# Modulation sums of two transformer layers moved from VectorE to GpSimd, gate columns made stationary, and up-projections of 512 columns

## The reference

```python
c_act = jax.nn.silu(c)
for l in range(DEPTH):                                   # 2
    mod = c_act @ w_mod[l] + b_mod[l]                    # [1024] @ [1024, 6144]
    shift1, scale1, gate1, shift2, scale2, gate2 = split(mod, 6)
    h = rms_norm(x, norm1) * (1.0 + scale1) + shift1
    proj = h @ w_in                                      # pooling, queries, keys, values, 24 gate columns
    mix = concat([pool_mixer(u), nsa_mixer(q, k, v, gates)]) @ w_out
    x = x + gate1 * mix
    h2 = rms_norm(x, norm2) * (1.0 + scale2) + shift2
    x = x + gate2 * (square(relu(h2 @ w_ff1)) @ w_ff2)   # 1024 -> 4096 -> 1024
```

## Time and profile before

| what | value |
|---|---|
| median of 3 runs (lowest, highest) | 1443.71 us (1436.76, 1446.1) |
| profiled execution | 1444.85 us, span 1443.2 us |
| mean granted clock of PE | 0.917 |
| heads of layer 0, and its feed-forward loop | about 125 to 197 us, 260 to 420 us |
| the same of layer 1 | about 520 to 586 us, 650 to 815 us |
| second block | from about 822 us |

### The profile page before, as it was taken

The page is one execution under the profiler, slowest core; times in us unless marked ns, Lnnn a source line. Parts: engine busy times, 40 slices in busy tenths (PEclk is TensorE's granted clock), DMA queues, the critical chain, the costliest instruction groups (busy, mean ns, idle before and its releaser), DMA issues.

```text
span 1443.2 us, 23428 instructions
## 1 busy us (share of the span) xinstructions
PE 1336.0 (93%) x9578; PEld 1228.0 (85%) x9578; DVE 920.0 (64%) x1435; ACT 629.1 (44%) x935; POOL 36.5 (3%) x39
## 2 busy tenths in 40 slices
PE   6798889999999987899999999898879999799997
PEld 6785468999998854789999998788759998799996
DVE  5747854677766579556544747987784753645553
ACT  3433213444435333144444444458876632644442
POOL 1012000000000120000000000000000000000000
PEclk8788659999999887799999999899979999899999
DMA  9451522676743515245555563336654361455540
GB/s 383 138 198 59 204 88 88 233 296 231 296 167 134 200 60 211 80 184 207 174 178 190 217 213 128 99 138 218 219 175 174 119 221 42 169 188 193 179 145 30
DMA packets 43626, 247.75 MB, mean 172 GB/s; under 512 B 4160, under 2 KB 12368, under 8 KB 15520
## 3 DMA queue, kind: packets, MB, share of 16 engines
q1 hardware_dynamic: 43104, 244.57, 47.4%
q0 software_dynamic: 448, 2.14, 0.4%
HBM read 245.58 MB, written 1.11 MB: 171 GB/s over the span
## 4 chain that ended last, share of the span: by engine, by line
PE 67%; DVE 14%; issue 12%; DMA 3%; ACT 3%; POOL 1%; SPq 0%; POOLq 0%; DVEq 0%; ACTq 0%
PE bank L331 20%; PE bank L332 19%; PE bank L333 19%; DVE arena L823 3%; DVE w_lo L326 2%; PE bank L407 2%; DVE arena L1662 1%; DVE arena L950 1%; DMA arena<-dscr 1%; DMA arena<-in_modw 1%; POOL arena L341 1%; ACT w_hi L321 1%; PE bank L1273 1%; PE bank L1316 1%; DMA cst<-in_cst 1%
## 5 line engine op out<-in xcount | busy, mean ns | idle before, releaser
L326 DVE TENSOR_TENSOR w_lo<-raw,w_hi 128x2048 fp32r<-128x2048 f32 x170 | 389.7, 2295 | 240.3 <-ACT w_hi L321 240.2
L331 PE MATMUL bank<-act_hi,w_hi 128*128 128x256 f32 x1568 | 467.2, 298 | 19.6 <-DVE act_lo L844 12.6
L332 PE MATMUL bank<-act_lo,w_hi 128*128 128x256 f32 x1568 | 455.4, 290 | 0.0
L333 PE MATMUL bank<-act_hi,w_lo 128*128 128x256 f32 x1568 | 454.8, 290 | 0.0
L321 ACT ACTIVATE w_hi<-raw 128x2048 fp32r<-128x2048 f32 x170 | 324.3, 1910 | 217.0 <-PE bank L333 117.4
L331 PEld LDWEIGHTS bank<-act_hi,w_hi 128*128 128x128 f32 x1568 | 312.7, 199 | 33.6 <-issue 28.5
L332 PEld LDWEIGHTS bank<-act_lo,w_hi 128*128 128x128 f32 x1568 | 313.9, 200 | 1.1 <-issue 1.0
L333 PEld LDWEIGHTS bank<-act_hi,w_lo 128*128 128x128 f32 x1568 | 313.0, 200 | 0.0
L331 PE MATMUL bank<-ff_hi,w_hi 128*128 128x256 f32 (+1 forms) x816 | 232.2, 285 | 2.9 <-DVE ff_lo L1046 1.9
L333 PE MATMUL bank<-ff_hi,w_lo 128*128 128x256 f32 (+1 forms) x816 | 231.4, 284 | 0.0
L332 PE MATMUL bank<-ff_lo,w_hi 128*128 128x256 f32 (+1 forms) x816 | 231.3, 283 | 0.0
(11 more groups left out here) (281 smaller groups left out, 1581.2 us busy)
## 6 DMA issues: line engine op xcount, KB each, us to landing
raw<-in_panels SPq DMA_DIRECT2D x170, 1024.0 KB, 4.9
arena<-in_modw SPq DMA_DIRECT2D x48, 1024.0 KB, 6.7
mixf<-dscr SPq DMA_DIRECT2D x8, 512.0 KB, 5.7
arena<-dscr SPq DMA_DIRECT2D x8, 512.0 KB, 4.6
mixf<-dscr SPq DMA_DIRECT2D x8, 256.0 KB, 6.1
...
arena<-in_x SPq DMA_DIRECT2D x1, 1024.0 KB, 5.2
```

What stands on the lines that cost most here:

```text
L326: nc.vector.tensor_tensor(w_lo[slot(k)][:, :], raw[:, k % RAW, :], w_hi[slot(k)][:, :].bitcast(F32), ALU.subtract).then_inc(lo_done, 1)
L331: nc.tensor.matmul(o, wh, xh, start=start, stop=False, skip_group_check=skip)
L332: nc.tensor.matmul(o, wh, xl, start=False, stop=False, skip_group_check=skip)
L333: return nc.tensor.matmul(o, wl, xh, start=False, stop=stop, skip_group_check=skip)
```

## The change

Three edits. The modulation sums of both layers (not the three pairs ahead of layer 0) go to POOL: four products of 512 columns in place in the unit, one add of 1024 columns, one of 512, and for a second half one more of 512. POOL's loop over layers is written out, and the sums stand behind `pool_window` in its program. The gate columns become the stationary operand, are copied to SBUF, and turned back by two transposes. Up-projections keep `act_hi` and `act_lo` side by side (`act2`), so that `w_hi` meets both in one matmul of 512 columns, and half `c` now has a bank of its own; ACT copies the cross part, DVE adds it to the other part, and takes ReLU and square in one instruction.

```diff
@@ -105,7 +105,8 @@
         w_hi = [sb(f"w_hi{i}", [P, PANEL], F32R) for i in range(SPLIT)]
         w_lo = [sb(f"w_lo{i}", [P, PANEL], F32R) for i in range(SPLIT)]
         x = sb("x", [P, KC, T])
-        act_hi, act_lo = sb("act_hi", [P, KC, T], F32R), sb("act_lo", [P, KC, T], F32R)
+        act2 = sb("act2", [P, KC, 2, T], F32R)
+        act_hi, act_lo = act2[:, :, 0, :], act2[:, :, 1, :]
 
         with nc.sbuf_tensor("mixf", [P, 2 * KC * T], F32) as mixf:
             pass
...
         ff_full = sem("ff_full")
-        ff_relu = sem("ff_relu")
+        ff_cross = sem("ff_cross")
+        ff_sum = sem("ff_sum")
         ff_sq = sem("ff_sq")
         ff_his = sem("ff_his")
         ff_ready = sem("ff_ready")
...
 
+        def pool_mods(pool, l, link):
+
+            for n in range(6):
+                for half in range(2):
+                    pool_mod(pool, 12 * l + 4 + n, mod_sums[:, 2 * n:2 * n + 2, :], half, link)
+
+            for pair in range(12 * l + 10, 12 * l + 16 if l + 1 < layers else 12 * l + 12):
+                pool.wait_ge(macc_free, 2 * pair + 2)
+                for half in range(2):
+                    pool_mod(pool, pair, macc[:, :, :], half, link)
+
+        def pool_mod(pool, pair, o, half, link):
+
+            pool.wait_ge(modraw[half], 16 * pair)
+            unit = modw[:, half, :].rearrange("p (b k n) -> p b k n", b=2, k=4)
+            for k in range(4):
+                kc = 4 * half + k
+                ins = nc.gpsimd.tensor_scalar(unit[:, :, k, :], unit[:, :, k, :], cact[:, kc:kc + 1], None, ALU.mult)
+            link(ins)
+            link(nc.gpsimd.tensor_tensor(unit[:, :, 0:2, :], unit[:, :, 0:2, :], unit[:, :, 2:4, :], ALU.add))
+            if half == 0:
+                nc.gpsimd.tensor_tensor(o, unit[:, :, 0, :], unit[:, :, 1, :], ALU.add).then_inc(mod_used, 1)
+            else:
+                link(nc.gpsimd.tensor_tensor(unit[:, :, 0, :], unit[:, :, 0, :], unit[:, :, 1, :], ALU.add))
+                pool.wait_ge(mod_used, 2 + 2 * pair + 1)
+                nc.gpsimd.tensor_tensor(o, o, unit[:, :, 0, :], ALU.add).then_inc(mod_used, 1)
+
         def pe_gfree(pe, l, g):
...
             pe.wait_ge(gw_lo, l + 1)
-            for tt in range(TT):
-                for kc in range(KC):
-                    ts = slice(tt * P, (tt + 1) * P)
-                    last = mm3(G(3)[:, tt * 24:(tt + 1) * 24], act_hi[:, kc, ts], act_lo[:, kc, ts], gwh[:, kc, :], gwl[:, kc, :],
-                               kc == 0, kc == KC - 1)
+            for kc in range(KC):
+                last = mm3(G(3)[0:24, 0:T], gwh[:, kc, :], gwl[:, kc, :], act_hi[:, kc, :], act_lo[:, kc, :], kc == 0, kc == KC - 1)
             last.then_inc(gfull, 1)
             pe_gfree(pe, l, 4)
             pe_used(pe, pe_panel(pe, m, L_Q0, G(4), act_hi, act_lo))
+            pe.wait_ge(gfree[1], 7 * l + 3)
+            for tt in range(TT):
+                last = nc.tensor.transpose(bank[3][:, 24 * tt:24 + 24 * tt], gf[0:24, tt * P:(tt + 1) * P], ident[0:24, 0:24])
+            last.then_inc(g_turned, 1)
             turn(0)
 
             pe.wait_ge(tb_lo, l + 1)
...
 
-                pe.wait_ge(ff_relu, jn + 1)
-                last = pe_panel(pe, mm, k, bank[4 + par], act_hi, act_lo, arr)
+                pe.wait_ge(lo_done, 4 * mm + k + 1)
+                wh, wl = w_hi[slot(k)], w_lo[slot(k)]
+                for c in range(2):
+                    pe.wait_ge(ff_sum, 2 * jn + c + 1)
+                    for kc in range(KC):
+                        if c == 0 and arr:
+                            arr(kc)
+                        s = kc * 256 + c * P
+                        nc.tensor.matmul(bank[4 + c][:, :], wh[:, s:s + P], act2[:, kc, :, :], start=kc == 0, stop=False)
+                        last = nc.tensor.matmul(bank[4 + c][:, 0:T], wl[:, s:s + P], act_hi[:, kc, :], start=False, stop=kc == KC - 1)
+                    if c == 0:
+                        last.then_inc(ff_full, 1)
                 pe_used(pe, last)
 
             def down(mm, k, jn, par, first, final):
...
             act.wait_ge(gfull, 3 * l + 1)
-            nc.scalar.activation(gts[:, :, :], G(3)[:, 0:48].rearrange("p (t n) -> p t n", t=TT), ACT.Exp, scale=-1.0).then_inc(gfree[1], 1)
+            nc.scalar.activation(gf[0:24, :], G(3)[0:24, 0:T], ACT.Copy).then_inc(gfree[1], 1)
             used(L_Q0)
             nc.scalar.activation(tbuf[:, 2:4, :], G(4)[:, :].rearrange("p (b t) -> p b t", b=2), ACT.Square).then_inc(nr_sq, 1)
+            act.wait_ge(g_turned, l + 1)
+            nc.scalar.activation(gts[:, :, :], bank[3][:, 0:48].rearrange("p (t n) -> p t n", t=TT), ACT.Exp, scale=-1.0).then_inc(gate_e, 1)
             split_hi(act, m, 7)
 
             def roots(*js):
...
             def step(mm, jn, kf, par, kd, s, at):
-
-                act.wait_ge(split_free, SPLIT + 4 * mm + kf + 1)
-
                 act.wait_ge(ff_ready, jn + 1)
-                nc.scalar.activation(fr[par], bank[4 + par][:, :], ACT.Relu).then_inc(ff_relu, 1)
+                for c in range(2):
+                    if c == 0:
+                        act.wait_ge(ff_full, jn + 1)
+                    else:
+                        act.wait_ge(split_free, SPLIT + 4 * mm + kf + 1)
+                    nc.scalar.activation(fr[par][:, c * T:(c + 1) * T], bank[4 + c][:, T:2 * T], ACT.Copy).then_inc(ff_cross, 1)
                 if s[0] is not None:
                     split_hi(act, mm, s[0])
                 act.wait_ge(ff_sq, jn + 1)
...
 
-            dve.wait_ge(gfree[1], 7 * l + 3)
+            dve.wait_ge(gate_e, l + 1)
             link(nc.vector.tensor_scalar(gts[:, :, :], gts[:, :, :], 1.0, None, ALU.add))
             link(nc.vector.reciprocal(gts[:, :, :], gts[:, :, :]))
             link(nc.vector.tensor_scalar(gts[:, 0, 0:24:3], gts[:, 0, 0:24:3], cst[:, C_VALID:C_VALID + 1], None, ALU.mult))
...
 
-            def mod(half, steps=(0, 8)):
-
-                pair = half // 2
-                dve_mod(dve, 12 * l + 4 + pair, mod_sums[:, 2 * pair:2 * pair + 2, :], half % 2, steps=steps)
-
             maxima(0)
             maxima(1)
             weigh(0)
@@ -980,8 +1023,6 @@
                     split_lo(dve, m, 11)
                 if i + 2 < 8:
                     maxima(i + 2)
-                for half in ((0,), (1, 2), (3,), (4, 5), (6,), (7, 8), (9,), (10, 11))[i]:
-                    mod(half)
                 if i >= 2 and i % 2 == 0:
                     mixed((i - 2) // 2)
             mixed(3)
@@ -1004,7 +1045,7 @@
                     nc.vector.scalar_tensor_tensor(x[:, kc, :], bank[4 + i % 2][:, c * T:(c + 1) * T], modc[:, 16 + kc:17 + kc], x[:, kc, :],
                                                    ALU.mult, ALU.add).then_inc(x_ready, 1)
             dve_norm(dve, 2 * l + 1, KC, 24)
-            dve_ff(dve, m, L_FF, 16 * l, l=l, mods="ahead" if ahead else "tail")
+            dve_ff(dve, m, L_FF, 16 * l)
 
             if ahead:
                 dve.wait_ge(macc_free, 2 + 24 * l + 32)
...
-                dve_mod(dve, pair, macc, half)
+        def dve_ff(dve, m, k0, j0, final=False):
 
             def step(mm, jn, kf, par, kd, s, at):
-                dve.wait_ge(ff_relu, 2 + jn + 1)
-                nc.vector.tensor_tensor(fr[par], fr[par], fr[par], ALU.mult).then_inc(ff_sq, 1)
+                for c in range(2):
+                    dve.wait_ge(ff_cross, 2 * jn + c + 1)
+                    nc.vector.tensor_tensor(fr[par][:, c * T:(c + 1) * T], bank[4 + c][:, 0:T], fr[par][:, c * T:(c + 1) * T], ALU.add).then_inc(ff_sum, 1)
+                dve.wait_ge(ff_sum, 2 * jn + 4)
+                nc.vector.scalar_tensor_tensor(fr[par], fr[par], 0.0, fr[par], ALU.max, ALU.mult).then_inc(ff_sq, 1)
                 if s[0] is not None:
                     split_lo(dve, mm, s[0])
                 dve.wait_ge(ff_his, jn + 1)
                 nc.vector.tensor_tensor(ff_lo[:, par, :], fr[par], ff_hi[:, par, :].bitcast(F32), ALU.subtract).then_inc(ff_ready, 1)
-                mod(at, par)
                 if s[1] is not None:
                     split_lo(dve, mm, s[1])
 
...
         @block.gpsimd
         def _(pool):
-            link = Chain(pool, pool_links, 7)
+            link = Chain(pool, pool_links, 0)
 
             pool.dma_start(ccol[:, :], a["ccol"]).then_inc(c_loaded, 16)
             nc.gpsimd.memset(ub, 0.0)
             nc.gpsimd.memset(wb[0], 0.0)
             link(nc.gpsimd.memset(wb[1], 0.0))
-            link.first = link.n
-            with pool.Fori(0, layers) as l:
-                link.layer(l)
-
+            for l in range(layers):
                 pool.wait_ge(x_ready, 16 * l + 8)
                 pool.dma_start(lc[:, :], a["lcs"][l]).then_inc(lc_ready, 16)
                 pool_rope(pool, l)
                 pool_window(pool, l, link)
-                link.end()
+                pool_mods(pool, l, link)
             pool_second(pool)
 
         @block.tensor
```

17 lines of the change are left out of this document (5 added, 12 removed).

## The result

The changed kernel takes **1626.39 us** (median of four runs, 1619.79 to 1628.28) against 1444.9 us (1436.76 to 1448.04): the ratio is 1.1258, with a 95% interval of 1.12 to 1.1315. I had forecast 1475 us, range 1440 to 1540. The sign was right; the size was six times mine, 183 us of span (1443.2 to 1626.5) against 30.

What follows compares the result with a forecast made beforehand. PE was taken to bound the feed-forward, and the last modulation sum to decide when the heads' output projection starts. From 1444.85 us, 47 + 8 - 18 + 1 - 8 = +30 gave 1475 us, range 1440 to 1540.

Steps and rivals of the forecast that it cites:

- The price of the product: POOL's one-input product of 512 columns in the modulation sums: 0.78 us, between the memset's 0.48 and the in-place add's 1.27.
- A: Rival: POOL products at the memset's rate, loads setting 12 us a pair, kernel not slower, 1439 us; chance 0.20.
- The attention term: Heads of both layers: PE waits for POOL's last modulation sum, +19.6 us in layer 0 and +27.4 in layer 1, together +47.
- What I added for contention: Heads: DVE's instructions hold up POOL's sums, 8 us a layer added to POOL, bounds 4 and 16.
- The feed-forward of layer 0: Six loop iterations, each with one POOL pair partly excluded by DVE: +1.3 us an iteration, +8 us, low 0, high +44.
- The feed-forward of layer 1: Only two POOL pairs there, with long pauses: nothing added.
- The gates: Gate columns: 48 matmuls of 24 columns become 24 of 256, gaining 5.0 + 3.1 us: -8 us.
- Up-projections: Feed-forwards: three matmuls of 256 columns become one of 512 and one of 256, gaining 0.024 us a group: -18 us.
- my own sign that the term is wrong: If the last feed-forward, which has no sums, does not get 6 us shorter, the up-projection term is wrong.
- The drain's +1 us: The up-projections' new drain of ACT copies and DVE adds, thinly covered only at the start of each feed-forward: +1 us.
- B: Rival: POOL products cost 1.27 us like an in-place add, with full exclusion between POOL and DVE, 1575 us; chance 0.13.
- the end of all terms: Whole kernel: the ends of all terms taken together give 1430 and 1600 us.

Runs made afterwards that it cites:

- pe_edits: The changed kernel with all modulation sums back on DVE, keeping the gate-column and up-projection edits: 1433.5 us, ratio 0.9937 to the kernel before.
- halves_on_pool: pe_edits with the second half of each of the heads' pairs summed on POOL, by a two-input product: 1494.74 us, ratio 1.0362 to the kernel before.
- early_tail_loads: The changed kernel with the last two modulation units of layer 1's feed-forward loaded one loop iteration sooner: 1609.82 us, ratio 1.1123 to the kernel before.
- gates_only: The kernel before with only the gate columns made stationary: 1441.85 us, ratio 0.9986.

## Why the prediction was wrong

**The price of the product: the step that failed.** I put the one-input product between the memset and the in-place two-input add, "nearer the memset", and kept 1.27 us as the upper bound since it has "one input less to read". It costs 1.55 us, above both ends. The pair is 21.3 us and not 13.7, which is 6 x 7.6 = 46 us a layer in the heads. Rows of two other instruction forms were no bounds for this one. The Trainium skill (GPSIMD Engine Reference, Engine selection) expects one-input operations at roughly line rate; the trace disagrees for this form, 2.5 ns a column, and the rival by that price, A (1439 us), was furthest off. Its other half, two-input operations about twice slower, the trace bears out (1.17 against 0.684 us).

**The attention term** (+47) came out at +54.9 and +64.6 us in the table, which has the gates' gain in it, and at +64.3 and +61.1 us against pe_edits. With the right price my own sum gives: POOL starts at 131.56 us, six pairs of 21.3 end at 259.4; measured 260.6. POOL without a gap, PE released by it, and the end of the sums as the moment that decides were right. What I added for contention (8 us a layer on POOL) was charged to the wrong engine: in the heads POOL lost 1 us and DVE some 22. That cost nothing here, since POOL alone needs 129 us and DVE's loss lies beside them, as the prediction said; in halves_on_pool, where POOL's time did not cover it, it is what lost.

**The feed-forward of layer 0** (+8, bounds 0 and 44) measured +48.1. The structure was right: POOL's pair, PE's turn, and two thirds of DVE's 11.9 us on top. Against pe_edits, which has the same shorter matmuls, the sums cost 50.9 us. POOL needs 29.0 us = 21.2 + 7.8, and two thirds of 11.9 is 7.9. With 21.2 in place of 13.7 my formula gives 30.1 us an iteration against 23.2, so +41. The iteration shown took 31.55: 1.1 us more are the pause that POOL makes while it waits for `macc_free` (2.1 us, where I had put 0.95), 0.4 us the gaps between its instructions. These add 9 us in six iterations and make 50; the loop without the sums took 23.6 us in pe_edits, not 23.2, and the few us left over are not assigned.

**The feed-forward of layer 1**: "nothing" was wrong by 17 us (19 against pe_edits). I had looked at the pauses ahead of its two pairs and not at what follows the last: its units are issued behind a panel, and everything behind it is the end of the stage. early_tail_loads gives 15 us of it back.

**The PE edits.** Up-projections: -18 taken; 0.0125 us a group is 16 x 48 x 0.0125 = -9.6 us, and pe_edits shows -2.8 and -1.8 us in the first two feed-forwards. The last one, from its first up-projection to the norm's sum on PE, takes 189.4 us in place of 193.2. It did not get 6 us shorter, which was my own sign that the term is wrong. I had taken the rate from 256 columns at half clock; 512 columns at full clock keep 0.02 us of their own. The gates came near their price in layer 0: their last matmul starts at 69.65 us instead of 74.20. With the clock that stayed up behind them, gates_only reaches L526 9.1 us sooner in layer 0. Together they are worth 11 us, and in layer 1's heads, at a lower clock, 3.5 us are lost again. The drain's +1 us could not be told apart.

**The rivals.** B (1575 us) had the right mechanism, a dear product and exclusion, and even it was 51 us short. Against pe_edits the heads' sums cost 125 us where B had 111, the feed-forward of layer 0 51 where it had 44, the tail 19 where it had nothing, and the PE edits gave 11 us where it had 25. So at most some 21 us of its error lie in the bound of 1.27 us. The chance of 0.13 was too low and even the end of all terms (1600) lay below the measured time; an operation that the trace doesn't show deserves an open upper end.

Added up: 54.9 + 1.2 + 48.1 + 64.6 - 0.2 + 17.4 - 2.7 = 183.3 us, the difference of the spans.
